# Identity products ahead of TensorE's four waits in the routing of a one-core decoder trunk

## The reference

```python
xn = rmsnorm(h, norm_mix_w);  z = xn @ w_in          # 12,576 columns: two recurrent branches and two gates
y_hg, y_rw = hgrn2_branch(...), rwkv7_branch(...)
merged = sigmoid(zga) * (y_hg @ w_branch_hg) + sigmoid(zgb) * (y_rw @ w_branch_rw)
h = h + merged @ w_out
hn = rmsnorm(h, norm_ffn_w)
h = h + hier_moe(hn, ...)                            # below
out = rmsnorm(h, final_norm_w)

# hier_moe, cut to what matters here
g_logits = hn @ wg_r + bg_r;  g_sel = argmax(g_logits)       # one of 4 groups
e_logits = (hn @ we_r + be_r)[group g_sel];  top_k(..., 2)   # two of the 8 experts in it
# tokens are sorted by expert into blocks of slots; for each block xb of expert e:
ys = (silu(xb @ w_gate[e]) * (xb @ w_up[e])) @ w_down[e]     # 32 experts, 3 x 4 MB of weights each
out = segment_sum(ys * weight, token)
```

## Time and profile before

| | |
|---|---|
| median of 3 runs | 2667.76 us (2667.15 to 2670.15) |
| span of the profiled execution, first to last instruction | 2664.7 us |
| the median over that span | 3.06 us |
| TensorE busy | 2513.9 us, 94% |
| mean granted TensorE clock | 0.983 |
| DMA, mean over the span | 223 GB/s |

### The profile page before, as it was taken

One profiled execution on the slowest core, in us unless ns is written; L12 is line 12 of the kernel. 1 busy time (PEld: TensorE's weight loads), 2 busy tenths in 40 slices (PEclk: granted clock), 3 DMA queues, 4 the chain that ended last, 5 costly groups with the idle time before them and its releaser, 6 DMA issues.

```text
span 2664.7 us, 40374 instructions
## 1 busy us (share of the span) xinstructions
PE 2513.9 (94%) x15789; PEld 1692.5 (64%) x15789; DVE 1135.8 (43%) x1649; ACT 814.4 (31%) x1010; POOL 105.4 (4%) x136
## 2 busy tenths in 40 slices
PE   7999999999999999999999998899999989989896
PEld 6888888877787777787788876333333333333342
DVE  5333343344566666566444233333332223323334
ACT  6433344433443445444222222021111111111112
POOL 0000000000000000000000000000000000000000
PEclk9999999999999999999999999899999999999998
DMA  5333333333232222233754434999999999999995
GB/s 170 108 97 110 110 95 97 99 111 82 83 87 79 82 83 80 83 84 93 240 147 144 162 113 187 393 421 421 422 422 421 422 422 422 422 422 421 422 421 223
DMA packets 312384, 594.43 MB, mean 223 GB/s; under 512 B 17098, under 2 KB 238918, under 8 KB 260550
## 3 DMA queue, kind: packets, MB, share of 16 engines
q1 hardware_dynamic: 303372, 559.71, 57.3%
q0 software_dynamic: 8912, 33.22, 3.2%
HBM read 578.02 MB, written 24.64 MB: 226 GB/s over the span
## 4 chain that ended last, share of the span: by engine, by line
PE 77%; DMA 16%; DVE 3%; issue 1%; ACT 1%; SPq 0%; DVEq 0%; ACTq 0%
PE in_z L160 36%; DMA ex_w_up<-in_expert_w_up_dram 16%; PE bank L2408 11%; PE bank L2435 4%; PE mg_z_rw L152 1%; PE mg_z_rw L150 1%; PE mg_z_rw L151 1%; PE bank L2395 1%; PE in_z L152 1%; PE in_z L150 1%; PE in_z L151 1%; PE rw_b L1324 1%; DVE in_lo L192 1%; PE bank L2396 1%; PE in_z L1612 1%
## 5 line engine op out<-in xcount | busy, mean ns | idle before, releaser
L160 PE MATMUL in_z<-xn_hi,in_hi 128*128 128x512 f32 x1440 | 568.9, 395 | 4.7 <-DVE in_lo L192 3.2
L160 PE MATMUL in_z<-xn_hi,in_lo 128*128 128x512 f32 x1440 | 571.3, 397 | 0.0
L160 PE MATMUL in_z<-xn_lo,in_hi 128*128 128x512 f32 x1440 | 563.7, 391 | 0.0
L2408 PE MATMUL bank<-ex_w_gate,ex_xt_sb 128*64 128x512 f32 x768 | 359.2, 617 | 55.8 <-DMA ex_w_up<-in_expert_w_up_dram 54.9
L192 DVE TENSOR_TENSOR in_lo<-in_raw,in_hi 128x2048 fp32r<-128x2048 f32 x122 | 281.6, 2308 | 283.4 <-ACT in_hi L187 167.3
L2410 PE MATMUL bank<-ex_w_up,ex_xt_sb 128*64 128x512 f32 x768 | 360.1, 618 | 0.0
L160 PEld LDWEIGHTS in_z<-xn_hi,in_hi 128*128 128x128 f32 x1440 | 270.7, 188 | 65.1 <-issue 5.6
L160 PEld LDWEIGHTS in_z<-xn_lo,in_hi 128*128 128x128 f32 x1440 | 270.4, 188 | 57.6 <-issue 1.7
L160 PEld LDWEIGHTS in_z<-xn_hi,in_lo 128*128 128x128 f32 x1440 | 270.6, 188 | 55.3
L2408 PEld LDWEIGHTS bank<-ex_w_gate,ex_xt_sb 128*64 128x64 f32 x768 | 104.7, 142 | 278.1 <-issue 278.0
L2435 PE MATMUL bank<-ex_w_down,const 128*64 128x512 f32 x512 | 228.7, 600 | 2.4 <-ACT const L2321 0.6
(11 more groups left out here) (508 smaller groups left out, 3477.5 us busy)
## 6 DMA issues: line engine op xcount, KB each, us to landing
ex_w_down<-in_expert_w_down_dram SPq DMA_DIRECT2D x128, 1024.0 KB, 21.3
ex_w_gate<-in_expert_w_gate_dram SPq DMA_DIRECT2D x96, 1024.0 KB, 22.4
ex_w_up<-in_expert_w_up_dram SPq DMA_DIRECT2D x96, 1024.0 KB, 25.4
in_raw<-in_w_in_dram SPq DMA_DIRECT2D x91, 1024.0 KB, 5.7
in_raw<-in_w_out_dram SPq DMA_DIRECT2D x32, 512.0 KB, 4.7
ex_w_gate0b<-in_expert_w_gate_dram SPq DMA_DIRECT2D x16, 1024.0 KB, 19.2
ex_w_up0b<-in_expert_w_up_dram SPq DMA_DIRECT2D x16, 1024.0 KB, 23.4
rt_then_ex_w<-in_expert_w_gate_dram SPq DMA_DIRECT2D x16, 1024.0 KB, 22.1
```

The lines of the kernel that those rows point to most:

```text
L160: return pe.matmul(out, w[:, k, :], x[:, k, :], start=(n == 0), stop=(n == PASSES * KT - 1), skip_group_check=True)
L2408: pe.matmul(gate_up[low, :], x_t[:, k, halves[u]], w_gate[n][u][:, j, :], start=start, stop=stop, skip_group_check=True)
```

## The change

A helper issues products of the identity with itself into one PSUM tile that the routing no longer needs (`turn_ps[0]`, the first of the four that took the transposes). The first two waits are already met at that place; they order the products behind the last readers of the tile. Then 9 products stand ahead of the wait for `lgt_read`, 50 ahead of "mask", 5 ahead of "first" and 70 ahead of `turn_one`, whose first instruction is the wait for the first rows of x. Their results are read by nobody. No wait and no other instruction is taken out.

```diff
@@ phase_route, TensorE
             logits(i)
             if i + 2 < KT // 2:
                 turn(i + 2)
+        keep["idle_products"] = idle = lambda count: [
+            pe.matmul(turn_ps[0][:, 0:P], ident, ident, start=True, stop=True, skip_group_check=True) for _ in range(count)]
+        pe.wait_ge(h_t_ready, KT // 2)
+        pe.wait_ge(odd_ready, KT // 2)
+        idle(9)
         pe.wait_ge(lgt_read, 2)
         for t in range(TT):
             mm = pe.matmul(lg_ps[:, t, :], lg_t[:, t * P:(t + 1) * P], fold[:], start=(t == 0), stop=(t == TT - 1),
                            skip_group_check=True)
         mm.then_inc(pe_done, 1)
 
+        idle(50)
         after(pe, "mask")
...
         mm.then_inc(pe_done, 1)
+        idle(5)
         after(pe, "first")
         for t in range(TT):
             mm = pe.matmul(first_ps, of_first[:, t, :], in_first[:, t, :], start=(t == 0), stop=(t == TT - 1), skip_group_check=True)
@@ phase_experts, TensorE
             turn_two((3,))
             down(i, 1, first)
 
+        keep["idle_products"](70)
         turn_one(0, first_x_in, 16)
         pair(0, True)
```

## The result

The changed kernel takes 2683.07 us (median of 5, 2681.05 to 2684.97) against 2667.76 (2666.94 to 2670.15). The ratio is 1.0056, 95% interval 1.0045 to 1.0067: slower by 15.3 us of the medians. The forecast was slower, 2676.0, with a range up to 2681.0: the direction was right and the size too small by almost half, 8.2 us forecast for 15.3 measured.

The account below looks back on a forecast made before the run. The weights' DMA stream was taken as the bound: products outlasting the waits, less gains from full clock, end unit 0 8.27 us later, delaying the first waiting load; span 2664.7 + 8.3 = 2673.0, plus 3.06 gives 2676.0; range 2665.5 to 2681.

Parts of the forecast that it names:

- The stream sets the end: Experts' part: DMA engines are full, so a later first waiting load of weights delays the end microsecond for microsecond.
- Rival 4: Experts' part: the weights' stream has reserve and TensorE's 54.9 us of load waits swallow the 8.3; time 2667.8, chance 0.07.
- the hole's 1.9 us: Weights' stream before the first waiting load: 1.9 us of lost DMA, all that an earlier TensorE can give back.
- The price of a product: Each added float32 identity product on TensorE: two rows of 0.111 us, 0.222 us in all.
- Rival 1: Added products cost half, 0.111 us; unit 0 ends 4.3 us earlier and the hole closes: 2665.9, chance 0.12.
- 9, 50 and 5 products: Ahead of fold, ranks and first block: 2.00, 11.10 and 1.11 us, starting these 1.12, 6.07 and 5.20 us later.
- 70 products, 15.54 us, from 1668.30: Ahead of the gather's turn: products follow the first block and end at 1683.84, starting the turn 10.93 us later.
- TensorE is then never idle before the gather's turn: Routing, up to the turn: the products leave TensorE no idle time, so the clock is 2.4 GHz throughout.
- a clock that falls inside the products: The added products themselves run at 1.2 GHz; the end comes some 38 us later, about 2706; chance 0.03.
- The 3.06 us between span and median: Whole kernel: median 2667.76 over profiled span 2664.7; added to the forecast span 2673.0 to give 2676.0.
- Rival 2: Turn and scaling: short rows make the clock fall before unit 0, which loses up to 2.66 us; 2676.0 to 2678.7, chance 0.25.

Follow-up runs that it names:

- ten: Kernel before, TensorE unchanged; SyncE's first waiting load waits for the end of unit 1 of block 0 instead of unit 0: 2675.35 against 2668.47 us.
- four: Changed kernel with counts fitted to the waits: 3, 24, 2, then 13 ahead of the register load and 18 behind; 2667.93 against 2669.09 us for the kernel before.
- six: As four, but 26 products instead of 18 behind the register load and three more between turn and unit 0; 2665.92 against 2668.36 us for the kernel before.
- eight: Changed kernel with transposes as products, 26 of the last 70 ahead of the register load, 44 behind; 2666.95 against 2668.36 us for the kernel before.
- nine: As eight, but 56 transposes instead of 44 behind the register load; 2667.66 against 2668.47 us for the kernel before.
- seven: Changed kernel with its counts, each product a one-row transpose of the identity; 2667.67 against 2668.36 us for the kernel before.
- One: Changed kernel with 13 of the last 70 products ahead of the register load, 57 behind; 2679.56 against 2669.09 us for the kernel before.
- Five: Changed kernel with counts 3, 25, 3, none ahead of the register load and 35 behind; 2668.13 against 2668.36 us for the kernel before.
- three: Changed kernel with only the last 70 products, the 9, 50 and 5 left out; 2679.81 against 2669.09 us for the kernel before.

## Why the prediction was right in direction and too small

- **The stream sets the end: right.** Over a range of 17.2 us in the load, the distance behind it stays within 980.6 to 984.6 us, and ten moves the end with TensorE untouched. Rival 4 (the stream absorbs the delay) is out. On the early side the kernels four, six, eight and nine have the load 2.3 to 2.6 us earlier and 0.8 to 2.4 us less time; each interval holds 1, so that the hole's 1.9 us was gained is likely, not shown.
- **The price of a product: right.** 0.222 us forecast, 2 x 0.112 measured, and two rows. Rival 1 was a wrong price; seven is nearly its case. Its own sum would have failed too: it put unit 0 4.3 us earlier, and in seven unit 0 ends 0.5 us later, since the pause and the clock are missing in it as well.
- **9, 50 and 5 products: right.** From the logits' rows the fold starts at 4.04 (+1.18, forecast +1.12), the ranks at 16.10 (+6.17, forecast +6.07), the first block at 18.33 (+5.27, forecast +5.20).
- **The failed step: "70 products, 15.54 us, from 1668.30".** Two terms are missing in it. TensorE has a pause of its own ahead of them, 2.96 us, at the wait for the number of blocks and its register load; I had the program's line before me and took the first block's end for the products' start. And the clock does not stay up across it: 18.7 us for the 140 rows (1673.94 to 1692.66) and not 15.54, +3.2. Together 6.1 of the 6.3 us that lack at unit 0; unit 0 itself (3.58 for 3.48) is 0.1 of the rest. The rows of x had been there for some 12.6 us by then, where 6.65 were forecast. One confirms both terms: with the pause covered it is gone from the rows, and the rows take 16.03 us. Five agrees, less cleanly, as its counts differ from four's by more than the cover. The median is 7.1 us over the forecast, 0.8 more than unit 0 explains; the medians of the kernel before alone lie between 2667.76 and 2669.09, and I give it no cause.
- **"TensorE is then never idle before the gather's turn": wrong**, by the same omission, and with it my chance of 0.03 for a clock that falls inside the products. It fell just ahead of them and stayed down for their first 6.1 us, not throughout.
- **The 3.06 us between span and median: harmless, but no constant.** In the changed kernel every execution's time stands 1.9 to 2.0 us over its span; the 3.06 also held how far the profiled execution lay from the median. The forecast adds its 8.2 us to the median either way.
- **Rival 2 (the clock falls at unit 0): real, but not here.** It happened in one, three, four, six, seven, eight and nine, at a cost of 1.1 to 1.7 us each against the changed kernel's 3.58 us for unit 0, and not in the changed kernel nor in five. The rule of the Trainium skill, page "TensorE: Matmul & The Clock Gate", section "Part 4: PE-mode transpose", that transposes do not count for the clock, is not borne out for full ones: eight holds 1.00 over 8 us of them. Whether it holds for the turn's half-wide ones is open; they and the 0.87 us of scaling end in a fall seven times of nine. What decides between the seven and the two I did not settle; it is not the pause ahead of the products, which three and seven have as the two have it.

No version is faster than the kernel before by what can be measured. The best by its median is six (0.9994, 0.9985 to 1.0003).

## What to carry to other kernels

Before work is put into an engine's wait, list everything that the engine's own program has between its neighbours there, register loads and waits for loop counts too: a long wait hides them from the profile, and they come out as soon as it is filled. Size filler by recorded rows, not by instructions in the source (a float32 product is two). And ask first what the gap is worth: here the whole routing could give back only the 1.9 us in which the weights' stream stood still, while each microsecond of excess went to the end in full.

## What was not expected of the hardware

The identity's transposes hold the full clock as well as its products do, with half the time each; in seven the clock also rose from 0.50 to 1.00 (at 1667.0) while TensorE ran nothing but these transposes. After nearly the same pause the clock came back at different times: 6.1 us after the first product in the changed kernel (pause 2.96 us), 5.5 us in five (2.91 us), and 2.8 us in seven (2.92 us). Executions differ by some 4 us in the part ahead of the routing: the last logits' rows start between 1648.1 and 1652.3 us in these traces.
